# Fewer fetched rows taken around the spread, the rest behind it

## The reference

```python
q = (xb @ w_query).reshape(-1, PEER_HEADS, 2, PEER_QHALF)           # 8 heads, two halves of 128
s = jnp.einsum('thpd,pkd->thpk', q, sub_keys)                       # 128 keys in each half
sv, si = lax.top_k(s, PEER_TOPK)                                    # best 16 of each half
cand = sv[:, :, 0, :, None] + sv[:, :, 1, None, :]                  # 256 candidates
cidx = si[:, :, 0, :, None] * N_KEYS + si[:, :, 1, None, :]
top_s, top_p = lax.top_k(cand, PEER_TOPK)                           # best 16 experts of 16384
eidx = take_along_axis(cidx, top_p); g = softmax(top_s)
act = gelu(einsum('thkd,td->thk', u_tab[eidx], xb))
out = einsum('thk,thkd->td', g * act, v_tab[eidx])
```

## Time and profile before

| | us |
|---|---|
| median of 3 runs | 1613.38 |
| the profiled execution | 1615.82 |
| its span, first to last instruction | 1613.8 |
| TensorE busy (matmuls) | 1582.1 |
| VectorE busy | 1101.5 |
| GpSimd busy | 494.1 |
| mean DMA rate | 331 GB/s |

### The profile page before, as it was taken

The page is one execution under the profiler, slowest core; times in us unless marked ns, Lnnn a source line. Parts: engine busy times, 40 slices in busy tenths (PEclk is TensorE's granted clock), DMA queues, the critical chain, the costliest instruction groups (busy, mean ns, idle before and its releaser), DMA issues.

```text
span 1613.8 us, 30119 instructions
## 1 busy us (share of the span) xinstructions
PE 1582.1 (98%) x12128; PEld 1506.9 (93%) x12128; DVE 1101.5 (68%) x2478; ACT 209.5 (13%) x604; POOL 494.1 (31%) x423
## 2 busy tenths in 40 slices
PE   9999999999899999999999999999999999999997
PEld 7688899999899999998898888999999999999997
DVE  3373379998899998545537425999879989944441
ACT  2251221111011000000003312111211100000000
POOL 0000033335444456533300001333534435533310
PEclk9999999999999999999999999999999999999999
DMA  6304489999999999999984446999999999999991
GB/s 245 131 16 147 137 304 389 384 394 406 409 408 409 401 409 408 409 409 409 409 326 155 144 149 227 339 397 386 396 409 408 408 405 408 408 410 408 409 378 60
DMA packets 149979, 534.94 MB, mean 331 GB/s; under 512 B 17617, under 2 KB 20434, under 8 KB 149842
## 3 DMA queue, kind: packets, MB, share of 16 engines
q1 hardware_dynamic: 89938, 314.90, 50.7%
q0 software_dynamic: 59904, 218.13, 34.5%
HBM read 531.92 MB, written 1.05 MB: 330 GB/s over the span
## 4 chain that ended last, share of the span: by engine, by line
PE 79%; DVE 10%; DMA 8%; issue 3%; ACT 0%; DVEq 0%; SPq 0%; ACTq 0%; POOLq 0%
PE ps L267 37%; PE ps L1159 30%; DMA raw<-in_v_rows 6%; PE ps L1122 4%; DVE big L1322 3%; PE ps L728 2%; PE ps L279 2%; DMA big<-in_u_rows,big 2%; DVE big L1272 1%; PE ps L1501 1%; PE ps L738 1%; DVE big L1268 1%; PE ps L1433 1%; DVE big L1298 1%; DVE big L1300 1%
## 5 line engine op out<-in xcount | busy, mean ns | idle before, releaser
L267 PE MATMUL ps<-big,raw 128*128 128x160 f32 (+2 forms) x5104 | 798.5, 318 | 2.5 <-ACT big L1225 2.5
L267 PEld LDWEIGHTS ps<-big,raw 128*128 128x128 f32 x5104 | 751.5, 191 | 35.6 <-issue 3.1
L1159 PE MATMUL ps<-big,raw 128*128 128x160 f32 x4096 | 579.1, 301 | 6.5 <-DVE big L1154 2.3
L1159 PEld LDWEIGHTS ps<-big,raw 128*128 128x128 f32 x4096 | 559.6, 190 | 15.7 <-DMA raw<-in_v_rows 12.7
L1185 POOL DMA_INDIRECT big<-in_u_rows,big x208 | 250.3, 1203 | 733.4 <-DVE big L1308 376.5
L1339 DVE SCALAR_TENSOR_TENSOR big<-big 128x1024 f32<-128x1024 f32 x201 | 258.0, 1284 | 191.3 <-PE ps L1159 107.7
L1185 POOL DMA_INDIRECT big<-in_v_rows,big x208 | 240.5, 1156 | 320.6 <-DVE big L1339 255.1
L1322 DVE CUSTOM_DVE_ANT_0 big<-big 128x1024 f32<-128x1024 f32 x208 | 244.4, 1222 | 22.4 <-DMA big<-in_u_rows,big 19.8
L1225 ACT ACTIVATE big<-ps 128x160 f32<-128x160 f32 x256 | 77.4, 303 | 512.7 <-PE ps L267 474.0
L374 ACT ACTIVATE big<-h 128x272 f32<-128x272 f32 (+1 forms) x32 | 12.7, 419 | 645.8 <-DVE h L1414 597.3
L1268 DVE MAX8 big<-big 128x8 f32<-128x128 f32 (+1 forms) x99 | 33.5, 339 | 88.3 <-ACT big L1194 76.3
(11 more groups left out here) (173 smaller groups left out, 762.7 us busy)
## 6 DMA issues: line engine op xcount, KB each, us to landing
raw<-in_u SPq DMA_DIRECT2D x256, 512.0 KB
raw<-in_v_rows SPq DMA_DIRECT2D x256, 512.0 KB
raw<-in_query SPq DMA_DIRECT2D x32, 512.0 KB
raw<-in_lru_w SPq DMA_DIRECT2D x24, 512.0 KB
raw<-in_mla_down SPq DMA_DIRECT2D x17, 512.0 KB
raw<-in_mla_out SPq DMA_DIRECT2D x8, 512.0 KB
big<-in_u_rows,big POOLq DMA_INDIRECT x208
big<-in_v_rows,big POOLq DMA_INDIRECT x208
```

The source lines that it names most:

```text
L267: mm = pe.matmul(out, w[:, c * P:(c + 1) * P], x[:, c, :], start=(c == 0), stop=(c == DC - 1))
L1159: return pe.matmul(accumulator(c), w, act_w[:, i, :], start=start, stop=False, skip_group_check=True)
```

## The change

At each of the two places around the spread, in both layers, VectorE took nine rows. It now takes four at the first and three at the second. Nothing else is edited; `rows` goes on from whatever row is next, and the number of those left for the tail is worked out from what was taken. In layer 0 there are 11 fewer rows taken at the spread (7 for 18): 106 of the 112 u rows were taken before the second half's groups, now 95, and the tail has 89 rows where it had 78. In layer 1 the first half's groups could take only 36 rows before the u rows were used up, now 40, and the tail has 63 rows where it had 56.

```diff
-ROWS_PER_FIND, ROWS_AT_SPREAD, ROWS_PER_GROUP, LAST_ROW_TILE = 6, 9, 2, 118
+ROWS_PER_FIND, ROWS_IN_BUFFERS, ROWS_PER_GROUP, LAST_ROW_TILE = 6, (4, 3), 2, 118
@@ peer, VectorE, behind the first two spread tiles
-        n = rows(n, n + ROWS_AT_SPREAD)
+        n = rows(n, n + ROWS_IN_BUFFERS[0])
         dve.wait_ge(exped, 1)
@@ behind the last three spread tiles
-        n = rows(n, n + ROWS_AT_SPREAD)
+        n = rows(n, n + ROWS_IN_BUFFERS[1])
 
         dve.wait_ge(spread_done, 1)
```

## The result

The changed kernel takes 1640.12 us (median of 4 runs, 1638.76 to 1640.6) against 1614.31 us for the kernel before: 1.0159 times as long, 95% interval 1.0141 to 1.0176. Loaded again it was 1.0134 times the kernel before there (1.0118 to 1.0151). The forecast was 1622.6 us, 1609 to 1628. The side was right, the size was not: the kernel lost 21.6 to 25.7 us where 9.2 were forecast.

The account below looks back on a forecast made before the run. TensorE (busy 98%) and, from the first expert layer's search, full DMA engines bound the kernel. Last fold +7.1, clock +2.1, layer 1 0 gave +9.2 us on the median 1613.38: 1622.6 us, range 1609 to 1628.

Parts of the forecast that it names:

- The stall at the spread: Layer 0's spread and first scatter product: waits of 1.20 and 4.63 us go; with the clock, TensorE is 8.0 us ahead.
- The halt and its place: Layer 0: GpSimd fetches only eight rows past the last taken, so the row stream halts; six rows, 15.3 us, not fetched.
- (a): Layer 0's tail: rows catch up, taking more than half the stream, last fold 6.4 us earlier: 1607 us; chance 0.17.
- (b): Layer 0's tail: rows catch up in part or land soon, last fold within 2 us of before: 1611 to 1616; chance 0.11.
- (c): Layer 1 waits for tiles, or layer 0's tiles run dry at 412 to 425: another 5 us, 1628; chance 0.06.
- Where the halted rows' bytes went: Layer 0's tail: bytes go to tiles, tile waits shrink 7.3 of 12.7 us, TensorE reaches the last fold near 816.
- First term: Layer 0's last fold waits for row 223 and starts 7.1 us later than before.
- the landing: Layer 0's tail: row 142 lands 7.3 us after its issue into an almost empty queue; ends 4.0 and 8.9.
- Second term: After layer 0's last fold wait TensorE's clock drops: 2.1 us more, ends 0 or 4 us.
- Third term: Layer 1: no stall to gain, rows in time, 0 to 1.5 us of tile waits near tile 105, taken as 0.
- the second rival: Layer 0's tail: the moved rows' cost cancels, last fold within 2 us of before, 1611 to 1616; chance 0.11.
- the first: Layer 0's tail: the row stream takes more than half of the DMA engines and catches up, 1607 us; chance 0.17.

Follow-up runs that it names:

- layer 0 alone: New counts of four and three rows in layer 0 only, layer 1 keeping nine and nine, against the kernel before: 1.0109, 17.6 us longer.
- 7.4 to 8.3 alone: New counts of four and three rows in layer 1 only, layer 0 keeping nine and nine, against the kernel before: 1.0046, 7.4 us longer.

## Why the prediction was wrong in its size

The sum had three terms: the last fold 7.1 us later, 2.1 us of low clock, nothing from layer 1. Set on one start they measured 12.5 (11.5 and the 1.0 of the start), 3.8 and 9.5: 25.8 us for 9.2. The largest miss is layer 1.

**The stall at the spread: right.** TensorE waits for nothing there, its clock stays up (1.00 at 410 to 440 us, 0.89 before), and the second product starts 9.1 us earlier, 8.0 without the 1.0 of the start.

**The halt and its place: right.** GpSimd waits for VectorE twice between 397 and 422 us, 12.3 and 10.8 us:

```profile
396.11 0.94 POOL L1185 DMA_INDIRECT big<-in_u_rows,big  x1 [0.30 <-issue]
409.39 1.18 POOL L1185 DMA_INDIRECT big<-in_u_rows,big  x1 [12.34 <-DVE big L1322]
...
422.57 1.17 POOL L1185 DMA_INDIRECT big<-in_u_rows,big  x1 [10.77 <-DVE big L1322]
```

After it the rows come 2.58 us apart to the end ((841.13 - 637.64) / 79), and the wait stands at line 1501. Rivals (a) and (b) both fell, and the failure was on (c)'s side, which had 0.06 and a price of 5 us.

**Where the halted rows' bytes went: wrong, and hidden by luck.** That the wait is 20.0 us where 22 were said is no confirmation. The prediction gave the bytes that the halted rows left to the tiles, cut 7.3 us from the tile waits of layer 0's tail and had TensorE at the last fold near 816. It came at 842.47 - 20.01 = 822.5, after 13.1 us of tile waits, and the last row was late as well. TensorE kept only the gain from the stall: 419.8 us after it was ready for the spread for 427.2 before, 7.5 us. Of the six transfers that it counted as halted, four were made by neither queue (339 GB/s at 410 to 440). In layer 0 that cost nothing, since the fold waits for the row; in layer 1 the same step failed, and there it cost.

**First term mis-sized: the landing, 7.3 us.** The prediction took the latency of layer 1's row 44, fetched into an empty row queue, and called row 142's queue almost empty. It was not. Row 144 was issued at 625.12 and had at 637.64:

```profile
621.91 1.49 POOL L1185 DMA_INDIRECT big<-in_v_rows,big  x1 [0.30 <-issue]
...
625.12 1.11 POOL L1185 DMA_INDIRECT big<-in_v_rows,big  x1 [0.30 <-issue]
```

That is 12.5 us, and two rows back, at 2.58 us each, row 142 had landed by about 632.5, 10.6 us after its issue at 621.91. With layer 0 alone VectorE waited for row 142 itself, issued at 622.43 and had at 634.20, 11.8 us:

```profile
634.20 1.29 DVE L1339 SCALAR_TENSOR_TENSOR big<-big 128x1024 f32<-128x1024 f32 x1 [1.00 <-DMA big<-in_v_rows,big]
```

In the groups rows and tiles together ask for 4 x 1.28 = 5.13 of every 5.15 us, so even there fetches queue behind each other. 10.6 for 7.3 is 3.3 us, above the upper end of 8.9. The pace (2.576 for 2.554 over 79 rows) adds 1.7. Less the 0.5 us by which this trace issued row 142 sooner than the 622.45 of the prediction, that is the last fold at 842.5 for 838.0. A simpler sum comes as close: VectorE has as many rows landed and not taken when the tail begins as before (three, counted back from 637.64 and from 658.00; the prediction had four for two), so the last row is later by 11 x 2.56 less the 8.0 us that TensorE is ahead, 20.2 us from the same start, against 19.0 measured (841.13 + 1.0 - 823.18).

**Second term: the clock, 2.1 us.** It was taken from the time that the clock stayed low after a wait of 4.6 us. The fold (1.75 more) and the 48 matmuls behind it (2.05 more) lost 3.8 us. The prediction's end for it was 4. The length of the wait is not all that counts: with four rows moved a wait of 4.32 us at the same fold cost 3.1 us (840.85 - 829.38 = 11.5 us to the first square sum, for 8.36).

**Third term, the step that failed most: layer 1, taken at 0, end 1.5.** It measured 9.5 (7.4 to 8.3 alone). The deficit was worked out rightly, but it was set against most of ten slots landed. The first tile wait is at 1503.7, some 83 us or 38 tiles into the tail:

```profile
1503.73 2.20 PEld L1159 LDWEIGHTS ps<-big,raw 128*128 128x128 f32 x16 [0.19 <-DMA raw<-in_v_rows]
```

At the 0.045 transfers per us that are short by then, the reserve was 4 tiles, an estimate from these numbers; no row counts landed tiles. Whether the slots had not filled while the rows stood still at the spread, or were lost in the groups, which ask for all that the DMA engines give, stays open. From there each tile cost 0.34 us and the tail 8.0. The tail's two bounds were known, and the choice of the lower one was the step without a row under it.

**The load.** Some 4 us of the 25.7 may be between two loads of the same kernel; 21.6 would have been outside the range as well. The terms above are mostly read from one trace each and carry some 3 us of the same spread, the landing and the pace above all; the 9.5 us of layer 1 and the wait at the fold are far above it.

An engine goes round the queues that have work, by the Trainium skill, DMA: Bandwidth & Descriptors, section Queues, rings and completion order. The traces agree: the last 60 rows of layer 0 came 2.56 to 2.58 us apart in every one. The prediction said that this rule excludes the second rival; it bears on the first, which needs more than half of the engines, and more than on the second. The Trainium skill, same page, section Anatomy of one DMA, gives 2.0 us plus the bytes at 436 GB/s, 3.2 us for such a fetch. Here it took 10.6 to 12.5, and the measurement decides.

## What to carry to other kernels

Here two streams shared full DMA engines half and half (a row every 2.56 to 2.58 us, twice its 1.28), and the stream that halted on full buffers did not make up its time, though TensorE was 8 us ahead. So before work is moved behind a stall, look for the last consumer of its stream and its margin (here 6.5 us). An estimate from these numbers: n rows moved cost n x 2.56, less the 8.0 us gained and the 6.5 of margin, plus 3.8 of low clock once the fold waits. That is 0, 7.2 and 17.5 us for four, seven and eleven rows; measured were -1.3 (not told from 0), 6.8 and 17.6. It was put together after these runs and is not tested on another. Take a fetch's latency from a stretch as loaded as the one it will run in, and don't count landed reserves as full without a row that shows them.

## What the runs showed of the hardware

A wait of 20 us at the last fold cost 3.8 us of low clock behind it, and one of 4.3 us at the same place 3.1; one of 4.6 us before the first scatter product cost 2.0 (7.19 us from the first product to the second, 5.15 in the changed kernel). A fetch of 512 KB issued by GpSimd landed 7.3 us after its issue in layer 1 with an empty row queue (counted back from a later row), and after 10.6 to 12.5 us in a stretch at full DMA use. The kernel before took 1618.4 us on one chip and 1614.1 and 1614.5 us on two others (medians of 12, 13 and 25 runs). The changed kernel loaded twice was 1.0159 and 1.0134 times as long as it, with intervals that overlap; its traces had 339 and 348 GB/s in one stretch of 30 us, half a transfer, which is too little to explain the 4 us.
